# A split-float32 Trainium kernel: all hidden tiles of two blocks by seven block products, their weight sums shared by VectorE and GpSimd

## What is computed

```python
def swiglu_half(x, g, w_up, w_down):
    h = rmsnorm(x, g)
    gate, up = jnp.split(h @ w_up, 2, axis=-1)
    return x + 0.5 * ((jax.nn.silu(gate) * up) @ w_down)
def trunk(x, states, p):
    ...
    for l in range(DEPTH):
        x = swiglu_half(x, p['ffn1_norm'][l], p['ffn1_w_up'][l], p['ffn1_w_down'][l])
        y, st = mixer(rmsnorm(x, p['mix_norm'][l]), l, lb_all[l], p, tuple(s[l] for s in states))
        x = x + y
        x = swiglu_half(x, p['ffn2_norm'][l], p['ffn2_w_up'][l], p['ffn2_w_down'][l])
```

## Time and profile before

| | |
|---|---|
| median of 3 runs | 2846.6 us (2843.3 to 2848.44) |
| the profiled execution | 2846.17 us |
| its span, first to last instruction | 2844.4 us |
| mean granted clock of PE | 0.997 |
| instructions | 63198 |

### The profile page before, as it was taken

One profiled execution on the slowest core, in us unless ns is written; L12 is line 12 of the kernel. 1 busy time (PEld: TensorE's weight loads), 2 busy tenths in 40 slices (PEclk: granted clock), 3 DMA queues, 4 the chain that ended last, 5 costly groups with the idle time before them and its releaser, 6 DMA issues.

```text
span 2844.4 us, 63198 instructions
## 1 busy us (share of the span) xinstructions
PE 2810.3 (99%) x24828; PEld 2766.3 (97%) x24828; DVE 1689.4 (59%) x2419; ACT 950.6 (33%) x1616; POOL 1596.5 (56%) x1466
## 2 busy tenths in 40 slices
PE   8999999999999999999999999999999999999998
PEld 7999999999999999999999999999999999999998
DVE  8554677545553578383784637766454446783645
ACT  4221233123152425151452414330412523452433
POOL 6666676556654674525464352766565556734343
PEclk9999999999999999999999999999999999999999
DMA  5796835665654655353444433355665557453532
GB/s 191 199 247 191 237 101 182 170 154 155 185 167 111 189 163 162 117 175 110 126 144 140 156 120 109 121 169 169 160 181 153 161 151 186 148 170 118 158 123 78
DMA packets 196956, 444.27 MB, mean 156 GB/s; under 512 B 13464, under 2 KB 57664, under 8 KB 195904
## 3 DMA queue, kind: packets, MB, share of 16 engines
q1 hardware_dynamic: 107360, 281.09, 30.4%
q0 software_dynamic: 40128, 125.83, 18.7%
q10 hardware_dynamic: 49248, 34.28, 4.0%
HBM read 422.64 MB, written 144.35 MB: 199 GB/s over the span
## 4 chain that ended last, share of the span: by engine, by line
PE 93%; DVE 3%; ACT 1%; POOL 1%; issue 1%; ACTq 0%; DVEq 0%; PEld 0%; POOLq 0%
PE dense L723 60%; PE SA L783 15%; PE SB L783 11%; POOL Wl L588 1%; PE SA L998 1%; PE SA L915 1%; PE SA L859 1%; PE SA L1001 1%; PE SA L903 1%; PE SA L846 0%; PE SA L920 0%; POOL Wh L586 0%; PE SB L1005 0%; PE SA L848 0%; PE SA L855 0%
## 5 line engine op out<-in xcount | busy, mean ns | idle before, releaser
L588 POOL TENSOR_TENSOR Wl<-raw,Wh 128x512 fp32r<-128x512 f32 x620 | 854.0, 1377 | 51.8
L586 POOL TENSOR_SCALAR Wh<-raw 128x512 fp32r<-128x512 f32 x620 | 450.9, 727 | 672.8 <-PEq L728 445.8
L723 PE MATMUL dense<-Hh,Wh 128*128 128x272 f32 x2768 | 585.8, 293 | 15.2 <-POOLq L590 10.1
L723 PE MATMUL dense<-Hh,Wl 128*128 128x272 f32 x2768 | 573.9, 289 | 0.5 <-issue 0.5
L723 PE MATMUL dense<-Hl,Wh 128*128 128x272 f32 x2768 | 572.6, 288 | 0.0
L723 PEld LDWEIGHTS dense<-Hh,Wh 128*128 128x128 f32 x2768 | 435.0, 189 | 25.7 <-issue 16.2
L723 PEld LDWEIGHTS dense<-Hl,Wh 128*128 128x128 f32 x2768 | 436.7, 189 | 0.0
L723 PEld LDWEIGHTS dense<-Hh,Wl 128*128 128x128 f32 x2768 | 434.0, 189 | 0.8 <-issue 0.8
L651 POOL TENSOR_TENSOR Sl<-pair,Sh 128x512 fp32r<-128x512 f32 x120 | 173.7, 1465 | 421.8 <-ACT Sh L1088 421.0
L723 PE MATMUL dense<-Ah,Wh 128*128 128x272 f32 x1408 | 291.9, 289 | 0.8 <-DVE X L1814 0.7
L723 PE MATMUL dense<-Al,Wh 128*128 128x272 f32 x1408 | 290.7, 288 | 0.0
(11 more groups left out here) (473 smaller groups left out, 6317.4 us busy)
## 6 DMA issues: line engine op xcount, KB each, us to landing
raw<-wst SPq DMA_DIRECT2D x276, 512.0 KB, 3.7
w_sums<-wst POOLq DMA_DIRECT2D x36, 1536.0 KB, 13.3
w_sums<-wst POOLq DMA_DIRECT2D x18, 2048.0 KB, 16.8
pair<-wst SPq DMA_DIRECT2D x120, 256.0 KB, 3.5
pair<-w_sums SPq DMA_DIRECT2D x60, 512.0 KB, 3.7
wsum<-w_sums SPq DMA_DIRECT2D x60, 512.0 KB, 3.6
w_sums<-w_sums POOLq DMA_DIRECT2D x12, 1536.0 KB, 9.0
wsum<-wst SPq DMA_DIRECT2D x60, 256.0 KB, 2.5
```

Source lines behind the costliest of these rows:

```text
L586: pool.tensor_scalar(Wh[:, j, cs], raw[:, j, cs], 1.0, 0.0, ALU.mult, ALU.add).then_inc(glink, 1)
L588: pool.tensor_tensor(Wl[:, j, cs], raw[:, j, cs], f32(Wh[:, j, cs]), ALU.subtract).then_inc(glink, 1)
L723: mm = pe.matmul(out[:, a, 0:HALF], w[:, ring, w0:w0 + 128], x[:, k, a * HALF:(a + 1) * HALF], start=(k == 0 and n == 0), stop=(k == nk - ...
```

## The change

It takes the blocks two and three of the first feed-forward to pairs alone; the first block stays mixed (its first two hidden tiles dense, then three dense and three pairs by turns). So 14 "late" pairs, numbered 6 to 19, take the place of 7 dense hidden tiles and 7 pairs. All four engines now work one pair ahead there:

- SP loads the two weight tiles of a late pair into `pair` for an even number and into `raw` for an odd one, once all low parts of the pair before the last are made. The loads for the `w_down` tiles of a block wait until all low parts of that block's last pair are made. The first pair of the next block is loaded before them.
- DVE makes S1, S2 and S3 of the next pair (`late_sums`, S3 in place) ahead of U of this pair, and three low parts (A11, A12, S3).
- POOL makes the low parts of S2 and S1, then the sum S4, then the low parts of S4 and A22, and issues one of the transfers for `w_sums` per pair. For the first pair of a block it does so among the splits of the `w_down` tiles before it, after the second and after the third.
- ACT makes the seven high parts as in the other feed-forwards: six of them, S4 last, stand before the silu of this pair, A22 after it.
- The engines' counts are changed to fit. PE, ACT and DVE use the code of the other feed-forwards (`fast`, `products`), with the waits of the late pairs.

```diff
 FFN_PIECES = 2 * FF_TILES + 3 * KT
-HALF_FAST, FAST = FF_TILES // 2 - 1, FF_TILES - 2
+MIXED, FAST = FF_BLOCK // 2 - 1, FF_TILES - 2
+HALF_FAST = MIXED + FF_TILES - FF_BLOCK
 EXTRA = 2 * (FAST - HALF_FAST)
 FFN_TILES = FFN_PIECES - 2 * FAST
 FFN1_T0 = (-EXTRA, 0)
-UP_AT = (2, 18, 34)
-HALF_AT = (-1, 3, 7)
-DOWN_AT = ((4, 12, 20), (10, 26, 40))
+UP_AT = 2
+MIXED_AT = -1
+DOWN_AT = ((4, 12, 20), (10, 18, 26))
 FAST_AT = (0, FF_BLOCK - 2, 2 * FF_BLOCK - 2, FAST)
...
+LATE_DVE, LATE_POOL = (A11, A12, S3), (S2, S1, S4, A22)
+LATE0 = FAST_AT[1]
+LATE = HALF_FAST - MIXED
+PAIR0 = (MIXED - LATE0, HALF_FAST, HALF_FAST + FAST, HALF_FAST + 2 * FAST)
+LOW0 = [MIXED * HALF_DVE - LATE0 * len(LATE_DVE)] + [
+    MIXED * HALF_DVE + LATE * len(LATE_DVE) + FAST * DVE_LO * f for f in range(2 * DEPTH - 1)]
+POOL0 = [MIXED * HALF_POOL - LATE0 * len(LATE_POOL)] + [
...
+            return raw[:, t, c * 512:(c + 1) * 512] if odd else pair[:, 2 * t + c, :]
+        def late_slot(odd, q):
+            if q in (S1, S2, S4):
+                return wsum[:, (S1, S2, S4).index(q), :]
+            return late_block(odd, *{A11: (0, 0), A12: (0, 1), S3: (1, 0), A22: (1, 1)}[q])
+        def late_sum_no(i, a):
+            return MIXED * 4 + (a - LATE0) * 3 + i * 3
+        def late_landed(i, a):
+            if a % 2:
+                return raw_pair_in, (a - LATE0 - 1) * 16 + 32 + i * 16
+            return pair_in, a * 16 + 32 + i * 16
...
+            def lates_read(i):
+                sp.wait_ge(q_lo, ONE + LOW0[0] + i * len(LATE_DVE))
+                sp.sem_inc(pair_began, 1)
+                sp.wait_ge(q_lo_pool, ONE + POOL0[0] + i * len(LATE_POOL))
+                sp.sem_inc(pair_began, 1)
+            def load_late(i, source):
+                lates_read(max(i - 1, LATE0))
+                for t in range(2):
+                    if i % 2:
+                        sp.dma_start(raw[:, t, :], wst[source + t, :, :]).then_inc(raw_pair_in, 16)
+                    else:
+                        sp.dma_start(pair[:, 2 * t:2 * t + 2, :].rearrange("p a c -> p (a c)"),
+                                     wst[source + t, :, :]).then_inc(pair_in, 16)
             def half_ffn(p0):
                 for b, nf in enumerate((FF_BLOCK, FF_BLOCK, FF_LAST)):
                     off = b * 24
                         load(p0 + 1, 1, 1)
                         load_two(p0 + 2, 2)
                         sp.dma_start(kbuf[:, 0:2, 0:448], lvm_d).then_inc(consts_in, 16)
-                    with sp.Fori(1 if b == 0 else 0, nf // 2) as i:
-                        load_two(p0 + UP_AT[b] + i * 2, off + i * 4)
-                        load_pair(HALF_AT[b] + i, off + 2 + i * 4)
+                        with sp.Fori(1, nf // 2) as i:
+                            load_two(p0 + UP_AT + i * 2, off + i * 4)
+                            load_pair(MIXED_AT + i, off + 2 + i * 4)
+                    else:
+                        for i in range(FAST_AT[b] + 1, FAST_AT[b + 1]):
+                            if i == FAST_AT[b] + 1:
+                                sp.wait_ge(raw_free, p0 + DOWN_AT[1][b - 1] + KT + RAW)
+                                sp.sem_inc(pair_began, 1)
+                            load_late(i, off + 2 * (i - FAST_AT[b]))
+                    if b < 2:
+                        load_late(FAST_AT[b + 1], off + 2 * nf + KT)
+                    if b:
+                        lates_read(FAST_AT[b + 1])
                     with sp.Fori(0, KT // 2) as i:
...
+            def late_lows(i, parts=(0, 1)):
+                for q in LATE_POOL:
+                    if int(q in (S4, A22)) not in parts:
+                        continue
+                    pool.wait_ge(q_hi, (PAIR0[0] + i) * 7 + (q + 1))
+                    pool.tensor_tensor(Sl[:, q, :], late_slot(i % 2, q), f32(Sh[:, q, :]),
+                                       ALU.subtract).then_inc(q_lo_pool, 1)
+                    if q == S1:
+                        pool.wait_ge(w_sum, late_sum_no(i, 0) + 2)
+                        pool.sem_inc(sum_began, 1)
+                        pool.wait_ge(q_lo_pool, ONE + POOL0[0] + i * len(LATE_POOL) + 2)
+                        pool.tensor_tensor(wsum[:, 2, :], late_block(i % 2, 0, 1), wsum[:, 1, :],
+                                           ALU.add).then_inc(w_sum_pool, 1)
             def half_ffn(p0):
                 c = 0
                 for b, nf in enumerate((FF_BLOCK, FF_BLOCK, FF_LAST)):
                     if b == 0:
                         for t in range(4):
                             one(p0 + t)
-                    for i in range(1 if b == 0 else 0, nf // 2):
-                        one(p0 + UP_AT[b] + 2 * i)
-                        if b or i > 1:
+                    for i in range(FAST_AT[b] + 1, FAST_AT[b + 1] if b else 0):
+                        late_lows(i)
+                        sums(1, c)
+                        c += 1
+                    if b:
+                        sums(1, c)
+                        c += 1
+                    for i in range(1, nf // 2 if b == 0 else 0):
+                        one(p0 + UP_AT + 2 * i)
+                        if i > 1:
                             sums(1, c)
-                        one(p0 + UP_AT[b] + 2 * i + 1)
-                        if not b and i == 1:
+                        one(p0 + UP_AT + 2 * i + 1)
+                        if i == 1:
                             sums(1, c)
                         for q, src in ((S3, pair[:, 2, :]), (S4, wsum[:, 2, :]), (A22, pair[:, 3, :])):
-                            pool.wait_ge(q_hi, (HALF_AT[b] + i) * 7 + (q + 1))
+                            pool.wait_ge(q_hi, (MIXED_AT + i) * 7 + (q + 1))
                             pool.tensor_tensor(Sl[:, q, :], src, f32(Sh[:, q, :]), ALU.subtract).then_inc(q_lo_pool, 1)
                         sums(1, c + 1)
                         c += 2
                     for m in range(KT):
                         one(p0 + DOWN_AT[1][b] + m, nf * P)
+                        if b < 2 and m in (1, 2):
+                            late_lows(FAST_AT[b + 1], (m - 1,))
                         if b < 2 and m in (2, 5):
                             sums(1, c)
                             c += 1
...
-                    pe.wait_ge(prod_read, n * 5 + (5 if alternate else 2))
+                    pe.wait_ge(prod_read, n * 5 + (5 if mixed else 2))
...
-                        by_dve, by_pool = ((A11, S2, S1, A12), (S3, S4, A22)) if alternate else (BY_DVE, BY_POOL)
+                        by_dve, by_pool = ((A11, S2, S1, A12), (S3, S4, A22)) if mixed else (
+                            (LATE_DVE, LATE_POOL) if alternate else (BY_DVE, BY_POOL))
...
-                    if alternate:
-                        with pe.Fori(1 if b == 0 else 0, nf // 2) as i:
+                    if alternate and b == 0:
+                        with pe.Fori(1, nf // 2) as i:
                             for j in range(2):
-                                up(UP_AT[b] + j, i)
-                            fast(HALF_AT[b] + i)
+                                up(UP_AT + j, i)
...
+            def late_high(i, a, q):
+                n = PAIR0[0] + a + i
+                if q in (A11, A12, A22):
+                    act.wait_ge(*late_landed(i, a))
+                elif q == S4:
+                    act.wait_ge(w_sum_pool, (a - LATE0) + i + 1)
+                else:
+                    act.wait_ge(w_sum, late_sum_no(i, a) + {S1: 1, S2: 2, S3: 3}[q])
+                act.wait_ge(prod_done, n * 7 + (q + 1))
+                act.activation(Sh[:, q, :], late_slot(a % 2, q), ACT.Copy).then_inc(q_hi, 1)
...
-                        high(f, a + i + 1, A11)
-                        high(f, a + i + 1, S2)
+                        next_high(A11)
+                        next_high(S2)
                     act.wait_ge(ffn_lo, t - 1)
                     act.wait_ge(prod_done, 7 + n * 7 + 3)
                     act.activation(tmp[:, j, HALF:TOK], SB[:, 0, 0:HALF], ACT.Copy).then_inc(prod_copy, 1)
                     if ahead:
                         for q in (S1, A12, S3, S4):
-                            high(f, a + i + 1, q)
+                            next_high(q)
                     act.wait_ge(prod_read, n * 5 + 7)
                     act.wait_ge(pair_mid, n * 3 + 2)
                     act.activation(tmp[:, 4 + j, :], tmp[:, 4 + j, :], ACT.Silu).then_inc(silu_done, 1)
                     if ahead:
-                        high(f, a + i + 1, A22)
+                        next_high(A22)
                     if copies_next:
                         first_product(n + 1)
                     act.wait_ge(pair_mid, n * 3 + 3)
...
+                        for q in range(7):
+                            late_high(0, LATE0, q)
...
+            def late_sums(i, a):
+                n, odd, no = PAIR0[0] + a + i, a % 2, late_sum_no(i, a)
+                B = [late_block(odd, t, c) for t in range(2) for c in range(2)]
```

(27 more changed lines are left out.)

48 lines of the change are left out of this document (28 added, 20 removed).

## The result

The kernel after takes 2914.7 us (median of 5 runs, 2912.7 to 2917.8), the kernel before beside it 2846.4 us (5 runs, 2843.3 to 2848.4): a ratio of 1.0239, 95% interval 1.0228 to 1.025, or 68 us more. The forecast of 2896 us had the sign right and 50 of the 68 us; 2914.7 lies above the range's end of 2910. The profiled execution took 2913.2 us, 67.1 more than the one of before.

What follows compares the result with a forecast made beforehand. PE, busy 99% of the span, was taken as the bound. The terms -10.5 + 39.5 + 8.0 + 8.2 + 2.0 + 2.5 = +49.7 us on 2846.2 gave 2896 us, range 2858 to 2910.

Steps and rivals of the forecast that it cites:

- Term 1: Blocks two and three: twelve matmuls fewer for each of seven mixed passes replaced by two pairs, -10.5 us.
- term 2: Late pairs: DVE and POOL take longer than PE's 10.55 us a pair, so PE waits, +39.5 us (ends 6 and 70).
- The laying out: The four engines' queues set against each other for a late pair: 14.4 us, or 13.2 to 14.9 with shifted durations.
- The five meetings: Late pairs: POOL's five instructions each hold up DVE's chain, by 1.2, 0.8, 0.6, 0.8 and 0.6 us.
- Rival (a): DVE and POOL meet less, the loop through POOL's sum bounds at 11.06 to 12.5 us: 2859 to 2878 us, chance 0.22.
- rival (b): PE stays the bound in the late pairs, so the kernel gets faster: 2841 us, chance 0.08.
- The loop through POOL: Late pairs: the way from `hidden_lo` through POOL's sum S4 and ACT's silu, by which each pair starts the next, 11.06 us.
- Term 3: End of the first block: PE waits for POOL's late splits of `w_down` tiles, +8.0 us (ends 0 and 11).
- costed at nothing: Splits of 14 dense tiles leaving POOL, loads of 3.7 us asked for about 12 us ahead, and the `w_sums` transfers: no cost.
- Term 4: End of the second block: PE waits for the last hidden tile, held behind POOL's sum S4, 8.2 us (ends 2 and 11).
- The 2 us at the end of the third block: End of the third block: DVE's lag alone remains, costing 2 us.
- Term 5: PE's granted clock falls to a lower level after two long waits, 1.25 us lost behind one, +2.5 us in all.

Runs made afterwards that it cites:

- e3: Against the kernel after, DVE's low parts in late pairs read one operand from PSUM, true low parts left out: pairs of 12.5 to 12.6 us, 2895.4 us in all.
- e4: Against the kernel after, POOL's five late instructions cover 64 of 512 columns, the rest left out: pairs of 11.0 to 11.1 us, 2872.7 us in all.
- e5: Against the kernel after, SP asks for the first block's first two `w_down` tiles ahead of pair 6: 2907.5 us.
- e2: Against the kernel after, DVE makes all four weight sums, S4 included, and POOL none: pairs of 13.7 to 13.8 us, 2895.7 us in all.
- e14: The kernel before with 96 semaphore increments at the start of PE's program: 2863.4 us, ratio 1.0056.
- e12: The kernel before, unchanged, timed and profiled again: 2847.5 us, ratio 1.0006.

## Why the prediction was right in sign and short in size

**Term 1 (-10.5) and term 2 (+39.5): right.** Blocks two and three together cost 30.9 us, where the two terms gave 29.0. The laying out gave 14.4 and the trace shows 14.4; the 14.1 that I took, as a middle of 13.2 to 14.9, is 0.3 x 9 = 2.7 us too little. That the sum is closer than that is partly luck in block three: its last pair, costed 2.7 us over 10.55, took 10.5, and the pair before it took 16.5 behind a fall of the clock, 2.1 us more, which the term didn't have. The five meetings came at the five places named, within 0.1 us each, and e3 shows that they are meetings and no late inputs. Rival (a), fewer meetings, and rival (b), PE stays the bound, fall with the same rows; (b) would have been near with POOL's work away (e4). The loop through POOL adds up to 11.04 us, not 11.06, which changes nothing.

**Term 3 (+8.0) and "costed at nothing": this is the first step that failed.** The term's own wait is right: 6.6 us in e5 against 7.2. What failed is the sentence on loads, 3.7 us and "asked for about 12 us ahead". It was made for the loads of the pairs and never asked of the first `w_down` tiles, past which the load of pair 6 moved in SP's queue, nor of four loads that go out in a burst behind a `w_sums` transfer. They took 10 to 12 us, PE waited 5.4, and 3 to 5 remain net (e5). The rule behind the sentence, that a load asked for early is hidden, held for the pairs: DVE waited once for one, 1.2 us.

**Term 4 (+8.2): right.** PE waited 7.3 us for `hidden_lo`, and e2 shows by taking S4 off POOL that the wait hung on that sum: ACT's row for it,

```profile
292.75 0.63 ACT L1186 ACTIVATE Sh<-wsum 128x512 fp32r<-128x512 f32 x1 [10.82 <-POOL wsum L722]
293.29 0.64 ACT L1223 ACTIVATE tmp<-tmp 128x544 f32<-128x544 f32 x1
```

has the silu (L1223) right behind it, as laid out. The wait is 0.9 us under the forecast, and the fall of the clock behind it 1.1 over, so that the stage comes out at +10.2 against 9.4. The 2 us at the end of the third block did not appear.

**Term 5 (+2.5): mis-sized.** It counted two falls of 1.25 us. There were three where PE is the bound, and two of them cost more than the 1.25 of the earlier trace rows: 17, 11 and 19 matmuls, or 2.1, 1.4 and 2.4 us.

**The rest (+10.8 against 2): the second step that failed.** The sum took for granted that work which the change doesn't touch keeps its time. It lost 10.8 us, of which 7.3 are longer "issue" waits of PE, waits that end 2.2 to 2.8 us after a transfer of instructions starts, and e14, with e12 as its control, shows that idle instructions ahead of PE's program can cost this much by themselves. No row of before could have given this size; the row L915 <- issue of 2.2 us was there to say that such waits exist.

Excess by these steps: loads and first clock fall 5.1, pairs 1.9, end of block two 0.8, the rest 8.8, which makes 16.6 of span. With the excess of the last stage away, 2914.7 - 8.8 = 2905.9 us would have been within the range; with that of the loads away, 2909.6, just so.

## What to carry to other kernels

Before giving part of VectorE's work to GpSimd, add VectorE's instructions with two SBUF inputs and GpSimd's work on SBUF into one sum, and compare that with the time per pass: here 11.6 us against 10.55, and moving a sum back to VectorE made the pass shorter. When a load moves in a queue, follow what stands behind it, and cost a burst of loads by a burst and not by the median of lone ones. Where a change moves the time by a few parts in a thousand, time a version that only displaces the program before explaining the untouched part.

## What the runs showed of the hardware that I had not expected

A fall of the clock costs nothing where PE is not the bound: in block two one late pair takes 16.5 us, in part at the lower level, and the next 12.0, together 28.5, or 14.3 each. (In block three the pair of 16.5 is followed by the last one, 10.5.) In a `w_down` stage the 11 to 19 matmuls that did not run are lost.

An increment of a semaphore in PE's stream took 0.106 us each between stages (48 of them 5.05 and 5.13 us). At the front of the program 48 cost 1 us and 96 cost 5.4.

PE's instructions seem to come late at times: mostly in the mixers it stood for 0.4 to 4.0 us at a time for nothing else that the profile shows, each time until 2.2 to 2.8 us after a 16 KB transfer of instructions started.

96 idle instructions ahead of PE's program cost this kernel 11 us of 2847 in a part that they don't touch, twice the 0.2% that I took as what can be told from no change: the kernel before measured again agrees to 0.1%, but this one doesn't.
